# Layer norm over 384 channels inside a mixer: channel blocks summed on VectorE before the all-ones matmul, with the last group's norm placed later

## The reference

```python
def layer_norm(x, g, b):
    mu = jnp.mean(xf, axis=-1, keepdims=True)
    var = jnp.mean(jnp.square(xf - mu), axis=-1, keepdims=True)
    return ((xf - mu) * lax.rsqrt(var + LN_EPS) * g + b)
...
    proj = jnp.einsum('btd,de->bte', x, w_in) + b_in
    a_in = a_val * jax.nn.sigmoid(a_gate)
    a = causal_dwconv(a_ext, conv_a_w) + conv_a_b        # 384 channels, 31 taps
    a = jax.nn.silu(layer_norm(a, ln_a_g, ln_a_b))
    bo = multiscale_pool(b_ext, pos0, w_pool) * pool_scale
    co = c_bg * causal_dwconv(c_ext, conv_c_w)           # 384 channels, 3 taps
    y = jnp.einsum('bte,ed->btd', jnp.concatenate([a, bo, co], axis=-1), w_out) + b_out
```

## Time and profile before

| | |
|---|---|
| median of 3 runs | 892.48 us (891.86 to 898.78) |
| the profiled execution | 892.87 us, its span 891.2 us |
| granted TensorE clock, mean of the span | 0.961 |
| PE busy in the span | 821.7 us (92%) |
| DVE, ACT, POOL busy | 593.5, 442.1, 269.9 us |
| input projection and convolution | 0 to 235 us |
| output projection | 235.7 to 353 us |
| routing | 353 to 389 us |
| experts, then the last norm | 389.9 to 854.6, then to 891.2 us |

### The profile page before, as it was taken

How to read it: one execution, slowest core, us unless ns; L and a number is a source line. 1 busy time by engine, 2 the same in 40 slices (tenths; PEclk the granted TensorE clock), 3 DMA queues, 4 the chain that set the end, 5 groups by cost and what they waited for, 6 DMA issues and landing times.

```text
span 891.2 us, 12717 instructions
## 1 busy us (share of the span) xinstructions
PE 821.7 (92%) x4267; PEld 714.5 (80%) x4268; DVE 593.5 (67%) x738; ACT 442.1 (50%) x495; POOL 269.9 (30%) x260
## 2 busy tenths in 40 slices
PE   6999999999999999279999999999999999999930
PEld 6999999998788886258888888888888888888820
DVE  4189999966675564889988984139831441965287
ACT  4212232536632222528888885248833543857243
POOL 1433565472000000023443343114421231333254
PEclk9999999999999999569999999999999999999975
DMA  8211111103647321468999999329982473892466
GB/s 292 55 48 47 47 47 45 33 18 115 215 179 279 136 98 74 153 207 286 391 391 386 376 395 363 53 47 344 394 291 40 116 274 63 272 389 43 95 188 244
DMA packets 59550, 167.75 MB, mean 188 GB/s; under 512 B 6798, under 2 KB 25231, under 8 KB 55430
## 3 DMA queue, kind: packets, MB, share of 16 engines
q1 hardware_dynamic: 51318, 144.57, 43.7%
q0 software_dynamic: 8208, 22.87, 11.9%
HBM read 144.79 MB, written 28.76 MB: 195 GB/s over the span
## 4 chain that ended last, share of the span: by engine, by line
PE 87%; DVE 8%; DMA 2%; issue 1%; ACT 1%; SPq 0%; POOL 0%; ACTq 0%; POOLq 0%; DVEq 0%
PE PS L1626 31%; PE PS L1377 19%; PE PS L1643 15%; PE PS L1556 10%; PE PS L1355 6%; DVE C L1126 2%; DMA RAW<-in_w_up 1%; PE PS L1404 1%; PE PS L1527 1%; PE PS L1444 1%; DVE RAW L1294 1%; PE PS L1508 1%; DVE BIG L399 1%; DMA F<-in_x_prompt 1%; DMA F<-x_rows,MIX 1%
## 5 line engine op out<-in xcount | busy, mean ns | idle before, releaser
L1626 PE MATMUL PS<-BIG,TH 128*128 128x512 f32 x1248 | 296.7, 394 | 1.5 <-DVE TH L1282 1.5
L1626 PEld LDWEIGHTS PS<-BIG,TH 128*128 128x128 f32 x1248 | 234.1, 189 | 49.6 <-issue 1.9
L1377 PE MATMUL PS<-BIG,WD 128*128 128x352 f32 x1080 | 177.3, 325 | 0.0
L1377 PEld LDWEIGHTS PS<-BIG,WD 128*128 128x128 f32 x1080 | 174.9, 188 | 0.9
L340 DVE TENSOR_TENSOR BIG<-RAW,BIG 128x2048 fp32r<-128x2048 f32 x64 | 145.1, 2288 | 24.3 <-ACT BIG L944 24.3
L1643 PE MATMUL PS<-WD,TH 128*128 128x512 f32 x624 | 155.8, 399 | 0.2 <-DVE TH L1331 0.2
L1643 PEld LDWEIGHTS PS<-WD,TH 128*128 128x128 f32 x624 | 113.6, 189 | 22.5 <-issue 0.3
L944 ACT ACTIVATE BIG<-RAW 128x2048 fp32r<-128x2048 f32 x64 | 119.1, 1908 | 16.1 <-PE PS L1556 7.9
L292 DVE SCALAR_TENSOR_TENSOR PS<-RAW,C,PS 128x512 f32<-128x512 f32 x174 | 115.3, 748 | 0.0
L1556 PE MATMUL PS<-BIG,WD 128*128 128x512 f32 (+1 forms) x432 | 100.7, 392 | 1.7 <-DVE BIG L399 1.7
L1556 PEld LDWEIGHTS PS<-BIG,WD 128*128 128x128 f32 (+1 forms) x432 | 76.7, 179 | 22.7 <-issue 1.3
(11 more groups left out here) (213 smaller groups left out, 772.8 us busy)
## 6 DMA issues: line engine op xcount, KB each, us to landing
RAW<-in_w_gate SPq DMA_DIRECT2D x64, 512.0 KB, 7.3
RAW<-in_w_up SPq DMA_DIRECT2D x64, 512.0 KB, 9.1
MIX<-in_w_down SPq DMA_DIRECT2D x32, 1024.0 KB, 10.4
F<-in_w_in SPq DMA_DIRECT2D x17, 512.0 KB, 4.1
F<-in_x_prompt SPq DMA_DIRECT2D x10, 512.0 KB, 4.8
x_rows<-F SPq DMA_DIRECT2D x9, 512.0 KB, 2.7
sum_rows<-F SPq DMA_DIRECT2D x9, 512.0 KB, 3.6
RAW<-in_w_out SPq DMA_DIRECT2D x4, 1024.0 KB, 6.3
```

The source lines that it names most:

```text
L1377: mm = pe.matmul(bank(3 * q + g, GRP), win[:, q, ws, c, :], xT[:, xs_, c, g * GRP:(g + 1) * GRP], start=(c == 0 and ws + xs_ == 0), stop=( ...
L1626: mm = pe.matmul(bank(h), xe[:, xs_, c, :], w, start=(c == 0 and xs_ + ws == 0), stop=(c == KD - 1 and xs_ == 1))
```

## The change

- VectorE adds the three channel blocks of the convolution's result once (`conv_sum`, 1056 columns, in the place of `gs`), and for each group the three blocks of squares (`sum_squares(g)`, into `stdev[g]`). `summed` is one matmul in place of three, for m0 to m2 and v0 to v2.
- `square(g)` may overwrite the squares when `sum_squares(g - 1)` is done, no more when v(g - 1) is.
- `tap_products(2)` on ACT stands behind `square(1)` (it stood behind `square(0)`) and waits for m2, since it writes where `conv_sum` lies.
- v2 leaves `project(N_BG + 1, 1)` and stands in `project_last`, behind p00 and p10; the history and pooling jobs of `project_last` move one block later.
- `deviation(2)` on ACT stands behind `mix_hi(0)`, `norm_a(2)` on DVE behind `mix_lo(0)`.
- `short_mul(0)` on DVE stands between the first two sums of squares.

```diff
+        conv_sum = F2[:, 0:TOK]
...
-                   ("c0", "state_out_bc", 1), ("c1", "state_out_bc", 2), ("v2", "stdev_a", 3),
-                   ("p00", "pool_out", 1), ("p10", "pool_out", 2), ("b01", "state_out_bc", 4), ("b2", "state_out_bc", 5)]
+                   ("c0", "state_out_bc", 1), ("c1", "state_out_bc", 2),
+                   ("p00", "pool_out", 1), ("p10", "pool_out", 2), ("v2", "stdev_a", 3), ("b01", "state_out_bc", 4), ("b2", "state_out_bc", 5)]
...
                 if g > 0:
-                    misc_ready(act, f"v{g - 1}")
+                    act.wait_ge(S("squares_summed"), g)
...
             square(0)
-            tap_products(2)
             state_a(0)
             state_a(1)
             act.wait_ge(S("win_lo"), NCH)
             deviation(0)
             square(1)
+            misc_ready(act, "m2")
+            tap_products(2)
             state_a(2)
...
             state_out("c1", out_cp, HC, WC, "state_out_bc")
-            deviation(2)
...
             mix_hi(0)
+            deviation(2)
             state_b()
...
+            dve.wait_ge(S("conv_taps"), 2 * TAPS * CA)
+            dve.wait_ge(S("sample_conv"), 2 * CA)
+            dve.wait_ge(S("gate_mul"), 2 * (CA + CC))
+            dve.tensor_reduce(conv_sum, mix[:, 0:CA, :].rearrange("p c t -> p t c"), AX, ALU.add
+                              ).then_inc(S("conv_summed"), 1)
+
+            def sum_squares(g):
+                dve.wait_ge(S("squared"), g + 1)
+                dve.wait_ge(S("win_lo"), NCH)
+                dve.tensor_reduce(stdev[g], squares.rearrange("p c t -> p t c"), AX, ALU.add
+                                  ).then_inc(S("squares_summed"), 1)
...
+            sum_squares(0)
             short_mul(0)
+            sum_squares(1)
             norm_a(0)
+            sum_squares(2)
             norm_a(1)
             short_mul(1)
+            short_mul(2, (0,))
+
+            mix_lo(dve, 0)
             norm_a(2)
-            short_mul(2, (0,))
-
-            mix_lo(dve, 0)
...
-                for c in range(CA):
-                    mm = pe.matmul(o[:, 0:GRP], ones, src(c), start=(c == 0), stop=(c == CA - 1))
-                mm.then_inc(S("misc_done"), 1)
+                pe.matmul(job(name)[:, 0:GRP], ones, src, start=True, stop=True).then_inc(S("misc_done"), 1)
...
-                                   state("c1", CC, lambda c: cP[:, c, SEQ:])), (variance(2),)))
+                                   state("c1", CC, lambda c: cP[:, c, SEQ:]))))
...
-                between = {1: (state("b01", CB, lambda c: sequences(bS, c, 0, nb0),
+                between = {1: (variance(2),),
+                           2: (state("b01", CB, lambda c: sequences(bS, c, 0, nb0),
                                      lambda c: sequences(bS, c, nb0, DECB - nb0)),),
-                           2: (state("b2", CB, lambda c: bP[:, c, SEQ:]),),
-                           3: (pool_linear(0, 1), pool_linear(1, 1)), 4: (pool_linear(0, 2), pool_linear(1, 2))}
+                           3: (state("b2", CB, lambda c: bP[:, c, SEQ:]),),
+                           4: (pool_linear(0, 1), pool_linear(1, 1)), 5: (pool_linear(0, 2), pool_linear(1, 2))}
```

More of the change, by code:

```diff
@@ L1105, in short_mul @@
                                              ).then_inc(S("short_done"), 1)
+            sum_squares(0)
             short_mul(0)
+            sum_squares(1)
             norm_a(0)
+            sum_squares(2)
             norm_a(1)
             short_mul(1)
-            norm_a(2)
             short_mul(2, (0,))
             mix_lo(dve, 0)
+            norm_a(2)
             wo_lo(dve, 0)
@@ L1441, in summed @@
             def summed(name, src):
-                o = job(name)
-                for c in range(CA):
-                    mm = pe.matmul(o[:, 0:GRP], ones, src(c), start=(c == 0), stop=(c == CA - 1))
-                mm.then_inc(S("misc_done"), 1)
+                pe.matmul(job(name)[:, 0:GRP], ones, src, start=True, stop=True).then_inc(S("misc_done"), 1)
             def turn_rows(name, *srcs, chunks):
@@ L1472, in run @@
                 def run():
-                    pe.wait_ge(S("conv_taps"), 2 * TAPS * CA)
-                    pe.wait_ge(S("sample_conv"), 2 * CA)
-                    summed(f"m{g}", lambda c: mix[:, c, g * GRP:(g + 1) * GRP])
+                    pe.wait_ge(S("conv_summed"), 1)
+                    summed(f"m{g}", conv_sum[:, g * GRP:(g + 1) * GRP])
                 return run
@@ L1479, in run @@
                 def run():
-                    pe.wait_ge(S("squared"), g + 1)
-                    summed(f"v{g}", lambda c: squares[:, c])
+                    pe.wait_ge(S("squares_summed"), g + 1)
+                    summed(f"v{g}", stdev[g])
                 return run
```

## The result

The changed kernel takes 896.99 us (median of 20 runs, 895.39 to 899.82), the kernel before 892.05 in the same runs (890.41 to 898.78). The ratio is 1.0055, with a 95% interval of 1.0045 to 1.0065: 4.9 us slower (4.0 to 5.8). The forecast was 898.0, 5.5 us above the median of before. The profiled execution took 896.44 us, its span 894.7.

What follows compares the result with a forecast made beforehand. PE was taken to bound the first stretch, with ACT nearly full in the second. Stalls 3.6 us plus slow clock 2.0 minus 0.1 gave 5.5 us slower: 898.0 us against the median, range 896.5 to 900.5.

Steps and rivals of the forecast that it cites:

- The PE work removed: Six means and variances on PE: about 9.6 us now, 2.8 with single matmuls, so 6.8 us removed.
- The reductions: Added DVE sums: conv_sum 5.0 us, hidden before PE's first mean, and sum_squares 1.8 us each.
- First stretch: First mean to last projection block: PE sheds 7.3 us, waits 8.0 (3.4 before v1, 2.9 before c0), ends 0.25 late.
- The list of waits and savings: First mean to last projection block: 7.3 us shed by PE against 8.0 us of waits, where it waited 0.2 to 0.3.
- the walk: Engines followed step by step from the first mean, at full clock: output projection starts 3.6 us late.
- Second stretch: Up to the output projection: ACT's late root and table loads delay swish(2) by 3.8 us, the output projection by 3.6.
- The clock: PE's clock falls in the little-work stretch 206.8 to 215.3; 4.8 us at half speed afterwards, costing about 2.0 us.
- the likeliest case: The forecast itself, 55%: PE's waits plus a fall of the clock in the stage, 898.0 us.
- The sum: Whole kernel: 3.6 + 2.0 - 0.1 = 5.5 us slower, 898.0 us against the median.
- rival 1: PE's stalls without the fall of the clock: +3.6 us, 896.1 us; chance 30%.
- Rival 3: a2's bank is free in time, so v1 and c0 don't wait: 1.8 us faster, 890.7 us; chance 4%.

Runs made afterwards that it cites:

- sums only: Kernel before with only the sums moved to VectorE (single matmuls), all other instructions at their old places: 889.58 us against 892.35, ratio 0.9974.
- Tap products only: Kernel before with tap_products(2) alone moved behind square(1), sums still by three matmuls: 897.77 us against 892.21, ratio 1.0065.
- filler run: Changed kernel with 18 matmuls into unused banks before v1's wait and 14 before c0's, results overwritten: 895.95 us, ratio 1.0042 against the kernel before.
- tap products back: Changed kernel with tap_products(2) put back behind square(0), still waiting for m2: 891.44 us against 892.35 for the kernel before, ratio 0.9998.
- late norm only: Kernel before with v2, deviation(2) and norm_a(2) alone moved to the late places, sums by three matmuls: 895.73 us against 892.35, ratio 1.0042.
- norm back: Changed kernel with v2, deviation(2) and norm_a(2) at their old places: 894.57 us against 892.35 for the kernel before, ratio 1.0029.

## Why the prediction was right

The change is slower, as forecast, by the mechanism forecast: ACT frees the banks of a2, a3 and p01 late, so PE waits, and the clock falls with the waits. The size was met with some luck, as the terms below show.

- **The PE work removed** was right: two means in 0.92 us (forecast 0.94), and 7.0 us less of PE in "sums only" (forecast 6.8).
- **The reductions** were priced too high: 3.83 and 1.37 us where I took 5.0 and 1.8. The step that was off is the choice of L1198 as the nearest row; a reduction across blocks costs 1.14 to 1.16 ns an element ((3828 - 156) / 3168 and (1365 - 156) / 1056), near the contiguous 1.03. The page "SBUF — State Buffer" of the Trainium skill (section "Door 1: The DMA port swizzle", note on cachelines) has a penalty for each new 16-byte line; if that is the difference, it is 0.12 ns an element here, and no run tries it apart. By the prediction's own terms the error is 0.5 us in the stage, towards slower.
- **First stretch.** v1's wait 3.25 (forecast 3.4), released by the copy of a2, as walked. "Tap products only" shows the cause by itself. c0's wait is 1.32 where I had 2.9, because PE came to it slowed by the clock; in the filler run, at full clock, 3.4 us lie between the end of the block and c0 (211.33 to 214.72), filled in part. GpSimd's two additions, which release a3 and so c0, take 5.36 us where I had 4.9; the last section says why. That gave back about what the cheaper reductions had gained: v1 comes 14.18 us after the first mean where I had 14.5, but c0 19.66 where I had 19.6. Without the slow clock (the filler run) PE's first-group matmuls come 23.35 us after the first mean, 0.21 later than before, where I had 0.25. This is luck, two errors that cancel. The list of waits and savings in the prediction adds up to 0.45 and not to the 0.25 that the walk gives.
- **Second stretch.** p02 waits 1.64 (1.6), and ACT waits 0.72 for the norm (0.6). The two table loads are there, each 1.28. The output projection waits 1.98, for which the forecast had no number. From `mix_hi(0)` to `wo_hi(0)` it is 10.17 us where it was 6.41, 3.76 more (I had about 3.7).
- **The clock** fell, as the likeliest case had it, but in the first of the two waits, and it was back at 218.4, not 220.1. It cost 1.56 us in the stage, by the filler run, where I had 2.0. (The prediction's terms, 4.8 us for work of 2.6, give 2.2; no row shows the 2.6.)
- **The sum.** 5.28 us in the stage, against 3.6 + 2.0 = 5.6, and 4.9 in time, against 5.5. The stage is 3.72 longer without the slow clock (the filler run), against 3.6, and the slow clock adds 1.56, against 2.0. So the clock's term was 0.4 too high, and the walk 0.1 too low. What I lacked is a possible second fall of the clock, behind the late norm's waits: three of the four profiles with these waits show it (tap products back, late norm only, filler), at 0.6 us each; the changed kernel's own doesn't.
- **The rivals.** The measured 4.9 us (4.0 to 5.8) takes in the forecast's 5.5 and lies above rival 1's 3.6 by little. The windows decide between them: the clock fell, and the filler run, which is rival 1's case, has 3.72 in the stage against its 3.6. Rival 3 (PE's saved work carries) needed a2's bank in time and kept the late norm. "Tap products back" is that case: v1 waits only 0.46 us and c0 not at all, yet it is only 0.2 us faster (0.92 in the stage), where rival 3 had 1.8. Its sum has no term for v0's wait of 1.98 us, which comes back with the tap products. Without the late norm its terms give 6.8 - 1.3 = 5.5 faster; "sums only" is 2.3.

Open: how long the clock is low from run to run, and how often the second fall comes. One execution of each kernel was profiled. The mean granted clock of the changed kernel's 20 runs goes from 0.954 to 0.959, so the slow stretches differ: the three runs at 0.959 took 895.50 to 895.65 us, the two at 0.954 took 898.99 and 899.75. In "norm back" (10 runs, 0.955 to 0.961) there is no such relation, so the clock's price in time is not settled by these numbers.

## What to carry to other kernels

Work taken off the busiest engine is worth only what the releases of its buffers allow: look at which engine copies out each small job, and at what stands ahead of that copy in its queue. Here 2.3 us of gain became 4.9 of loss by moving six activations ahead of one copy, and a root between two silus. On an engine that ends a stage, order the queue by when each result is needed (the silu of group 2 was needed five tiles later), and count a table load at both borders of a function that is moved alone. A TensorE wait can have a second price, the slow clock behind it: in all three kernels in which v1 waited 3.2 us with nothing to do (the change, norm back, tap products only) the clock fell in the wait or within 1.0 us after it, and in the changed kernel that cost 1.56 us of the stage.

## What the runs showed that I had not expected

In the changed kernel the three products of norm 0 take 5.86 us where they took 1.40. They lie beside GpSimd's two additions, which before ran beside other work of DVE or none. The timeline rows of DVE and of GpSimd, the first of the two additions in the kernel before, and one row of the line's own view (minimum, median, maximum in ns):

```profile
208.68 5.86 DVE L1107 TENSOR_TENSOR MIX<-MIX,F 128x352 f32<-128x352 f32 x3
```

```profile
208.80 2.68 POOL L633 TENSOR_TENSOR MIX<-MIX,F 128x1056 f32<-128x1056 f32 x1 [11.48 <-ACT F L830]
211.56 2.60 POOL L635 TENSOR_TENSOR MIX<-MIX,F 128x1056 f32<-128x1056 f32 x1
```

```profile
204.04 2.43 POOL L632 TENSOR_TENSOR MIX<-MIX,F 128x1056 f32<-128x1056 f32 x1 [6.14 <-ACT F L829]
```

```profile
L1107 DVE TENSOR_TENSOR MIX<-MIX,F x3: 524/2740/2750, 208.7 to 211.8; 128x352 f32<-128x352 f32 x3
```

The first product takes 0.52 us, the second and third 2.74 and 2.75, each as long as one addition of GpSimd. The Trainium skill, "SBUF — State Buffer", section "Who interferes with whom", says that a VectorE instruction with two SBUF inputs contends with a GpSimd instruction that reads SBUF, and calls the shared pair of ports an exclusive lock; the numbers agree, since each of the two late products ends some 0.4 us after an addition has ended (211.48 and 214.16), about the time that a product takes alone. On DVE it cost nothing, as DVE was waiting for `square(2)` until 216 anyway. On GpSimd it did cost something: from the start of the first addition to the end of the second it is 5.36 us (208.80 to 214.16), where the kernel before has 4.96 (204.04 to 209.00) and "tap products only", whose additions run beside no product, 4.92. The copy of a3 and the start of c0 follow at once (214.19 and 214.72), so c0 comes 0.4 us later by it. "Norm back" and the filler run show the same 5.86 and 5.91 us; in the kernels with the tap products at their old place the additions lie earlier, and the products take 1.40.
